# w_o and y of the RWKV projection loaded in the last head pair, without the meetings between; a weight ring of ten chunks

## What is computed

```python
for i in range(DEPTH):                      # DEPTH = 2
    h = rms_norm(x, norm_mix_g[i])
    mix = rwkv7_time_mix(h, ...) if i % 2 == 0 else mla_mix(h, ...)
    x = x + mix                             # both end in "... @ w_o", 1024 x 1024
    x = x + expert_choice_ffn(rms_norm(x, norm_ffn_g[i]), ...)

# the end of rwkv7_time_mix: y is normalised per head of 64
y = ((y - mean) * lax.rsqrt(var + GN_EPS)).reshape(b, s, d)
y = y * gn_g + gn_b + bonus.reshape(b, s, d)
out = (y * g) @ w_o

def expert_choice_ffn(h, w_router, w_gate, w_up, w_down):
    aff = jax.nn.softmax(h @ w_router, axis=-1)          # 512 x 16
    gates, idx = lax.top_k(jnp.swapaxes(aff, 1, 2), cap) # cap = 64 tokens an expert
    xe = h[b_idx, idx]
    hid = jax.nn.silu(xe @ w_gate) * (xe @ w_up)         # w_*: 16 x 1024 x 1024 a layer
    ye = (hid @ w_down) * gates[..., None]
    return jnp.zeros_like(h).at[b_idx, idx].add(ye)
```

## Time and profile before

| what | us |
|---|---|
| median of three runs (lowest, highest) | 2177.22 (2176.36, 2178.32) |
| the profiled execution, its time | 2174.74 |
| its span in the trace | 2172.6 |
| last pair's v projection done on PE, end of the pairs | about 663, 720 |
| layer 0: first matmul of the projection | 743.00 |
| layer 0: PE starts on chunk 0, last chunk read | 845.08, 1295.3 |
| layer 1: projection, PE starts on chunk 0, last chunk read | 1603.30, 1701.7, 2152.0 |
| PE busy (share of the span), mean clock | 1872.0 (86%), 0.955 |
| DVE, ACT, POOL busy | 845.8, 511.7, 228.6 |
| DMA moved, mean rate | 462.01 MB, 213 GB/s |

### The profile page before, as it was taken

The page is one execution under the profiler, slowest core; times in us unless marked ns, Lnnn a source line. Parts: engine busy times, 40 slices in busy tenths (PEclk is TensorE's granted clock), DMA queues, the critical chain, the costliest instruction groups (busy, mean ns, idle before and its releaser), DMA issues.

```text
span 2172.6 us, 43866 instructions
## 1 busy us (share of the span) xinstructions
PE 1872.0 (86%) x19382; PEld 986.8 (45%) x19382; DVE 845.8 (39%) x1685; ACT 511.7 (24%) x989; POOL 228.6 (11%) x264
## 2 busy tenths in 40 slices
PE   3689999999998595999888887699986799989987
PEld 2257766666667342333333324566643333333332
DVE  6557556564654114222212212477733222222211
ACT  1133443453343020111010101355521011001010
POOL 0031133033113020000000000111201000000000
PEclk8899999999999796999999998899998899999999
DMA  3111011011100744999999982200044599999996
GB/s 81 33 34 36 8 36 41 20 29 36 41 8 10 270 200 186 427 427 428 427 426 428 427 343 73 97 22 31 11 184 166 243 427 427 427 428 427 427 428 285
DMA packets 84534, 462.01 MB, mean 213 GB/s; under 512 B 16637, under 2 KB 49786, under 8 KB 59770
## 3 DMA queue, kind: packets, MB, share of 16 engines
q1 hardware_dynamic: 82042, 450.82, 50.8%
q0 software_dynamic: 2304, 8.39, 1.0%
HBM read 451.06 MB, written 8.13 MB: 211 GB/s over the span
## 4 chain that ended last, share of the span: by engine, by line
PE 60%; DMA 19%; DVE 6%; issue 6%; ACT 5%; DVEq 2%; SPq 1%; ACTq 1%; POOLq 0%; POOL 0%; PEldq 0%; another core or an unknown queue 0%
DMA arena<-in_moe_w_down 18%; PE banks L1504 14%; PE bank L602 7%; PE banks L1256 5%; PE banks L769 5%; PE bank L1504 4%; PE bank L1548 3%; PE banks L873 2%; PE banks L1548 2%; ACT arena L1936 2%; PE banks L956 1%; PE banks L459 1%; PE banks L893 1%; PE banks L747 1%; PE banks L1486 1%
## 5 line engine op out<-in xcount | busy, mean ns | idle before, releaser
L1504 PE MATMUL banks<-arena 128*64 128x512 f32 x2560 | 569.9, 598 | 32.7 <-DMA arena<-in_moe_w_up 20.3
L1504 PEld LDWEIGHTS banks<-arena 128*64 128x64 f32 x2560 | 179.0, 137 | 387.8 <-issue 338.4
L602 PE MATMUL bank<-arena 128*128 128x512 f32 x384 | 191.4, 626 | 9.1 <-ACT arena L642 8.0
L1605 DVE TENSOR_TENSOR arena<-arena,bank 128x512 f32<-128x512 f32 x80 | 55.0, 688 | 337.4 <-PE bank L1548 337.4
L1504 PE MATMUL bank<-arena 128*64 128x512 f32 x512 | 118.8, 610 | 38.7 <-issue 25.7
L1104 POOL TENSOR_TENSOR arena<-arena 128x512 f32<-128x512 f32 x80 | 101.6, 1295 | 436.5 <-DVE arena L1159 436.3
L769 PE MATMUL banks<-arena 64*64 64x64 f32 x5632 | 126.8, 221 | 10.1 <-issue 6.9
L769 PEld LDWEIGHTS banks<-arena 64*64 64x64 f32 x5632 | 111.0, 134 | 49.1 <-issue 40.7
L1256 PE MATMUL banks<-arena 128*128 128x512 f32 x256 | 115.3, 607 | 16.1 <-POOLq L379 16.1
L1593 DVE SCALAR_TENSOR_TENSOR arena<-arena,banks 128x512 f32<-128x512 f32 x32 | 33.7, 1053 | 212.6 <-PE banks L1504 212.6
L1560 ACT ACTIVATE arena<-banks 128x512 f32<-128x512 f32 x32 | 19.1, 598 | 413.0 <-PE banks L1504 413.0
(11 more groups left out here) (322 smaller groups left out, 2612.3 us busy)
## 6 DMA issues: line engine op xcount, KB each, us to landing
arena<-in_moe_w_gate SPq DMA_DIRECT2D x64, 2048.0 KB, 35.4
arena<-in_moe_w_up SPq DMA_DIRECT2D x64, 2048.0 KB, 35.4
arena<-in_moe_w_down SPq DMA_DIRECT2D x64, 2048.0 KB, 29.7
out_dram<-arena SPq DMA_DIRECT2D x12, 512.0 KB, 3.5
arena<-in_x SPq DMA_DIRECT2D x8, 512.0 KB, 11.4
arena<-in_rw_wr SPq DMA_DIRECT2D x8, 512.0 KB, 4.2
arena<-in_rw_wk SPq DMA_DIRECT2D x8, 512.0 KB, 6.0
arena<-in_rw_wv SPq DMA_DIRECT2D x8, 512.0 KB, 6.0
```

What stands on the lines that cost most here:

```text
L602: last = nc.tensor.matmul(b[:, :], w_sl[:, n, k, :], xmix[n][:, k, :], start=(k == 0), stop=(k == ND - 1))
L1504: last = nc.tensor.matmul(b[z * CAP:(z + 1) * CAP, :], st[:, k, :], ring[g % RING][:, k, z * 512:(z + 1) * 512], start=(c % 2 == 0 and k = ...
L1605: nc.vector.tensor_tensor(xs, xs, b[:, :], ALU.add).then_inc(free[COMB[j]], 1)
```

## The change

The regions. The ring has ten slots: seven at the arena's end, then `hT`, then `h_tok`, then the 4,096 floats ahead of `RING0`. What routing uses is placed in that last region (`fin`), and what the experts still need of it goes to the small array. For layer 0, w_o and yT get a place of their own over `xmix`, at the arena's end; this covers slots 3 to 6 of the ring.

The front. There are no meetings between the pairs and the projection of layer 0. In the last-but-one pair, once PE has done the v projection, SP issues w_o and, after six stores of y, their load. Pair 6's y goes straight into yT. PE does seven of eight k steps of the first job, the last y's transposes, seven of the second job, then the two last steps. The bank numbers of layer 0's projection go on from those of the pairs.

SP's order around the routing. Chunks 0 to 2 go first (in layer 0 after the last y), 3 and 4 ahead of the last row store (in layer 0 after the last out job), 5 to 7 after it, 8 when the row stores have landed, 9 when the slots have been made (in layer 0 also after a meeting in which SP now takes part, since the semaphores of the pairs are cleared there). At the end the four tiles of x are stored each after its last addition, with no meeting.

```diff
@@ -101,9 +101,10 @@
         ps = [banks06[:, b * 512:(b + 1) * 512] for b in range(6)]
         ps += [ctx.enter_context(nc.psum_tensor(f"bank{b}", [P, 512], F32)) for b in range(6, NB)]
 
-        RING0 = ARENA - (RING - 1) * CHUNK
-        ring = [arena[:, RING0 + s * CHUNK:RING0 + (s + 1) * CHUNK].rearrange("p (k n) -> p k n", k=4)
-                for s in range(RING - 1)]
+        KEPT = 7
+        RING0 = ARENA - KEPT * CHUNK
+        four = lambda v: v.rearrange("p (k n) -> p k n", k=4)
+        ring = [four(arena[:, RING0 + s * CHUNK:RING0 + (s + 1) * CHUNK]) for s in range(KEPT)]
         common = place(0)
         x_sb = common(NT, D)
 
...
@@ -192,12 +193,14 @@
         proj = place(AFTER_H + D)
         wo_sb = proj(ND, D)
         assert proj.at[0] <= RING0
-        yT = hT
+        early = place(ARENA - (3 * ND * S + 4 * S))
+        wo_at = [early(ND, D), wo_sb]
+        yT = [early(ND, S), hT]
 
         y_dram = a["out"][0].rearrange("(k q) (c s) -> k (q c) s", k=NPAIR, c=2)
 
 
-        moe = place(AFTER_H + D)
+        moe = place(AFTER_H)
         xeT = moe(ND, 2 * CAP)
         hidT = [moe(ND, CAP) for _ in range(2)]
         hid = [moe(512) for _ in range(2)]
...
@@ -996,10 +1001,8 @@
                         proj_piece(pe, rj, "v", u, n + 1)
 
         def last_y_pe(pe):
-            pe.wait_ge(ynorm_ready, 1)
-            for t in range(NT):
-                last = nc.tensor.transpose(ps[0][:, t * P:(t + 1) * P], ysq[:, t * P:(t + 1) * P], ident[:, :])
-            last.then_inc(full[0], 1)
+            pe.wait_ge(ynorm_ready, NPAIR)
+            turn(pe, ("yT", NPAIR), lambda m: ysq[:, m * P:(m + 1) * P])
 
         def y_square(act, n):
             act.wait_ge(ycen_ready, n)
...
@@ -1143,10 +1146,12 @@
             nc.vector.tensor_tensor(dst, ytok_flat, gT, ALU.mult).then_inc(ydone_ready, 1)
 
         def last_y_dve(dve):
+            for h in range(2):
+                job_read(dve, rj, ("y", h, NPAIR - 1))
             y_centre(dve)
-            y_variance(dve, 1)
-            y_scale(dve, 1)
-            y_finish(dve, 0, 1, 1, yT[:, NPAIR - 1, :])
+            y_variance(dve, NPAIR)
+            y_scale(dve, NPAIR)
+            y_finish(dve, *rj[("yT", NPAIR)], (NPAIR - 1) % 2, yT[0][:, NPAIR - 1, :])
 
         def pairs_dve(dve):
             for u in range(NPAIR):
...
@@ -1242,20 +1247,21 @@
         for t in range(NT):
             order += [(("out", t, z), (2 * t + z) % 4) for z in range(2)]
             order += [(("tr", t, i), 4 + i) for i in range(2)] + [(("lg", t), 6 + t % 2)]
-        oj = Jobs(order + [("sel", 0), ("at", 1), ("st", 2)])
+        order += [("sel", 0), ("at", 1), ("st", 2)]
+        ojs = [Jobs(order, rj.count), Jobs(order)]
         tile = lambda t: slice(t * P, (t + 1) * P)
 
         def out_pe(pe, n):
+            oj = ojs[n]
             pe.wait_ge(ld_wo[n], 16)
-            if n == 0:
-                pe.wait_ge(ld_y, 16)
-
-            def out(t, z):
-                b = open_job(pe, oj, ("out", t, z))
-                for k in range(ND):
-                    last = nc.tensor.matmul(b[:, :], yT[:, k, tile(t)], wo_sb[:, k, z * 512:(z + 1) * 512],
+
+            def out(t, z, ks=range(ND)):
+                b = open_job(pe, oj, ("out", t, z)) if 0 in ks else ps[oj[("out", t, z)][0]]
+                for k in ks:
+                    last = nc.tensor.matmul(b[:, :], yT[n][:, k, tile(t)], wo_at[n][:, k, z * 512:(z + 1) * 512],
                                             start=(k == 0), stop=(k == ND - 1))
-                last.then_inc(full[oj[("out", t, z)][0]], 1)
+                if ND - 1 in ks:
+                    last.then_inc(full[oj[("out", t, z)][0]], 1)
 
             def turn_x(t):
                 pe.wait_ge(x_ready, t + 1)
...
@@ -1282,8 +1288,19 @@
                 if t == NT - 1:
                     last.then_inc(full[oj["sel"][0]], 1)
 
-            out(0, 0)
-            out(0, 1)
+            if n == 0:
+
+                pe.wait_ge(ld_y, 16)
+                pe.wait_ge(ydone_ready, NPAIR - 1)
+                out(0, 0, range(ND - 1))
+                last_y_pe(pe)
+                out(0, 1, range(ND - 1))
+                pe.wait_ge(ydone_ready, NPAIR)
+                for z in range(2):
+                    out(0, z, range(ND - 1, ND))
+            else:
+                for z in range(2):
+                    out(0, z)
             pe.wait_ge(router_ready, 1)
             for t in range(1, NT):
                 out(t, 0)
...
@@ -1441,7 +1461,7 @@
             nc.vector.tensor_copy(token_f, token_i)
             b = job_full(dve, oj, "st")
             nc.vector.tensor_copy(slot[:, :, 0:NE], b[:, 0:NT * NE].rearrange("p (t e) -> p t e", t=NT))
-            dve.drain()
+            dve.drain().then_inc(routed[layer], 1)
             picks(dve, 0)
 
         def picks(dve, first):
...
@@ -1623,14 +1644,29 @@
 
         def load_experts(sp, layer):
 
-            for g in range(RING - 1):
+            if layer == 0:
+                sp.wait_ge(ydone_ready, NPAIR)
+            for g in range(3):
                 load_chunk(sp, layer, g)
             rows = h_dram.rearrange("(t p) d -> p t d", p=P)
             for t in range(NT):
+                if t == NT - 1:
+                    if layer == 0:
+                        job_full(sp, ojs[0], ("out", NT - 1, 1))
+                    load_chunk(sp, layer, 3)
+                    load_chunk(sp, layer, 4)
                 sp.wait_ge(h_done[layer], t + 1)
                 sp.dma_start(rows[:, t, :], h_tok[:, t, :]).then_inc(h_stored[layer], 16)
+            load_chunk(sp, layer, 5)
+            load_chunk(sp, layer, 6)
             sp.wait_ge(hT_read[layer], 1)
-            load_chunk(sp, layer, RING - 1)
+            load_chunk(sp, layer, KEPT)
+            sp.wait_ge(h_stored[layer], 16 * NT)
+            load_chunk(sp, layer, KEPT + 1)
+            if layer == 0:
+                meet(sp, "sp")
+            sp.wait_ge(routed[layer], 1)
+            load_chunk(sp, layer, KEPT + 2)
             for g in range(RING, CPP * PAIRS):
                 chunk_read(sp, layer, g - RING)
                 load_chunk(sp, layer, g)
...
@@ -2027,9 +2063,7 @@
             meet_pool(pool, [consts_ready])
             meet_pool(pool, prep_sems, everyone)
             pairs_pool(pool)
-            meet_pool(pool, pairs_sems, everyone)
-            y_rstd(pool, 1)
-            meet_pool(pool, banks + y_sems, everyone)
+            y_rstd(pool, NPAIR)
             for layer in range(2):
                 if layer == 1:
                     norm_pool(pool)
...
@@ -2041,9 +2075,13 @@
                     attn_pool(pool)
                     meet_pool(pool, attn_sems, everyone)
                 out_pool(pool, layer)
-                meet_pool(pool, route_sems)
+                if layer == 0:
+                    meet_pool(pool, route_sems + [x for x in pairs_sems if x not in banks], everyone)
+                else:
+                    meet_pool(pool, route_sems)
                 moe_pool(pool, layer)
-                meet_pool(pool, moe_sems, everyone)
+                if layer == 0:
+                    meet_pool(pool, moe_sems, everyone)
 
         @block.tensor
         def _(pe):
...
@@ -2056,9 +2094,6 @@
             first_pe(pe)
             meet(pe, "pe")
             pairs_pe(pe)
-            meet(pe, "pe")
-            last_y_pe(pe)
-            meet(pe, "pe")
             for layer in range(2):
                 if layer == 1:
                     norm_pe(pe)
...
@@ -2153,9 +2187,10 @@
             pair_loads(sp, 0)
             gate_loads(sp, 0)
             meet(sp, "sp")
+            wo = [a[w][0].rearrange("(k p) n -> p k n", p=P) for w in ("rw_wo", "mla_w_o")]
             pair_loads(sp, 1)
             for u in range(NPAIR):
-                if u:
+                if 0 < u < NPAIR - 1:
                     sp.wait_ge(ydone_ready, u)
                     sp.dma_start(y_dram[u - 1], y_out[u % 2]).then_inc(y_stored, 16)
                 sp.wait_ge(full[rj[("g", u)][0]], rj[("g", u)][1])
...
@@ -2164,18 +2199,16 @@
                     sp.wait_ge(full[rj[("v", u)][0]], rj[("v", u)][1])
                 if u < NPAIR - 2:
                     pair_loads(sp, u + 2)
-            sp.wait_ge(y_stored, 16 * (NPAIR - 1))
-            sp.sem_inc(waited_sp, 1)
-            meet(sp, "sp")
+                if u == NPAIR - 2:
+                    sp.dma_start(wo_at[0], wo[0]).then_inc(ld_wo[0], 16)
+                    sp.wait_ge(y_stored, 16 * (NPAIR - 2))
+                    sp.dma_start(yT[0][:, 0:NPAIR - 2, :], y_dram[0:NPAIR - 2].rearrange("k p s -> p k s")).then_inc(ld_y, 16)
             sp.wait_ge(ld_pair, LOADS * NPAIR)
             sp.wait_ge(ld_gate, 16 * 2 * NPAIR)
-            sp.dma_start(yT[:, 0:NPAIR - 1, :], y_dram[0:NPAIR - 1].rearrange("k p s -> p k s")).then_inc(ld_y, 16)
-            wo = [a[w][0].rearrange("(k p) n -> p k n", p=P) for w in ("rw_wo", "mla_w_o")]
```

(5 more changed lines are left out.)

63 lines of the change are left out of this document (34 added, 29 removed).

## The result

The changed kernel took 2139.35 us (median of four runs, 2135.06 to 2141.43) beside 2177.06 for the kernel before (four runs); the ratio is 0.9826, 95% interval 0.9811 to 0.9840, 37.7 us less. A repeat with five runs gave 2138.11 and 0.9815 (0.9802 to 0.9829), 39.7 us less. The profiled execution took 2135.06, its span 2133.3.

A forecast was written before the change was run, and what follows sets the result against it. It took DMA streaming expert weights at 427 GB/s as the main bound, besides SP's queue before the projection. Terms summed to -44.9 us, from 2174.74 to 2129.8 profiled; with 2.5 to the median, 2132.3, range 2127 to 2143.

The forecast's parts named there:

- five signs of being wrong: PE idle before job three; first gather 8 us or more; expert DMA below 420; w_down not ending the chain; longer last pair.
- late router: Rival, layer 0's projection: router columns or x come late, PE stands before job three up to 4 us; 2136 us, chance 0.11.
- crowding: Rival, routing: both first gathers pay the whole 6.2 us and PE or DVE stands once per layer; 2147 us, chance 0.12.
- signs of being right: Projection near 720 without cold stretch, second job 735.2, chunk 0 near 823, refill to landing 435 us, last addition 4 before end.
- The front: Pairs to layer 0's projection: early w_o and y loads and no meetings bring the second job forward, -24.7 us.
- The first gather of layer 0: Routing, layer 0: the gather meets the chunk stream for some 4 us and lands when it drains, +2.0 us, bounds 0 and 6.2.
- The ring: Expert stages: ten chunks resident at the first read leave two fewer to stream, -9.8 us in each layer.
- The first gather of layer 1: Routing, layer 1: the gather meets the end of chunk 9's transfer, +1.0 us, bounds 0 and 6.2.
- The end: End of the span: three tiles' stores go ahead and only the last is left after the last addition, -3.9 us.
- slower rival: Expert stream: ten transfers in flight run at a lower rate than eight; 2226 us at 10% less, chance 0.02.

The follow-up runs named there:

- wo_late: The changed kernel with w_o loaded after the last y matmul, not under the last pair: 9.3 us slower than the changed kernel on the same chip.
- wo_twice: The changed kernel with w_o loaded twice in the last pair, the second time when the first has landed: 34.9 us less than the kernel before.
- ring8: The changed kernel with a ring of eight slots in place of ten: 24.6 us less than the kernel before.
- end_meet: The changed kernel with the last meeting back and the four stores of x behind it: 34.4 us less than the kernel before.
- before_a: The kernel before, unaltered, timed and profiled once more: 2180.24 us.
- before_b: The kernel before, unaltered, timed and profiled yet again: 2181.18 us.

## Why the prediction was right, and where it was off

The range, 2127 to 2143, held both medians, and the path of the forecast is the one that happened. But the time lies 7 us above the forecast of 2132.3, and two of the five signs of being wrong were seen: a first gather of 8 us or more (9.7), and a last pair longer because of its loads. The range held because it had been drawn wide for a late router, which didn't come, and for most of the crowding, which came in part; that the cost of the w_o load, for which no case had a price, fitted into it too is luck. The signs of being right came in kind, each up to some 6 us late: the first projection matmul at 723.6 without a cold stretch, the second job taken at 738.2, PE on chunk 0 at 828.6, the last addition 3.1 us before the end; from the first refill to the last landing are 435.4 and 435.6 us, as said. By its own steps:

1. The front. Forecast -24.7 from the shift of the second job. Counted from the y copy it is 15.1 in place of 40.25, -25.1; PE didn't stop, the clock stayed at 1.00, and the router was ready 2.8 us ahead of job three, so "late router" didn't come. What failed is the sentence that 13.6 us of transfer "lie under that work": the cover costs. The step gave the w_o load no price, and it measured +3.8 us (66.7 against 63.0), shown by wo_late and wo_twice. PE waits there for blocks of its code that land late.
2. The first gather of layer 0. Forecast +2.0 with bounds 0 and 6.2; measured 8.7 to 9.7 in six kernels with chunk 9 beside it against 4.4 to 4.7 in eight without, +4.5. The step reasoned that it meets the stream for only some 4 us and lands when that drains. The queue was longer than that: chunk 8 was to be in at about 813 and landed at 819.68, 3.4 us of that from the later y copy, and chunk 9 at 825.5, where 818 was said. So the gather had 9.3 us of stream beside it, and landed 0.3 us behind chunk 9 (0.3 to 0.6 in all six kernels). The Trainium skill, "DMA: Bandwidth & Descriptors", section "Queues, rings and completion order", lets each engine take turns between its rings packet by packet. The prediction worked out +1.2 us from equal shares, saw that the median of 10.8 is far above that, and supposed unequal packets without putting a size to them. The trace has the size: a packet of the chunk is four times as large as one of the gather (14 and 3.6 KB above). Turns of one packet each would put 2.0 MB of chunk beside the gather's 0.52, 4.8 us at 427 GB/s; that is an estimate, and it is near the +4.5. In its timing the trace agrees only in part: the gather's packets are spread over 4.6 us in place of 2.3, but the first of them also starts late, 4.7 us after the issue in place of 1.9 (4.3 to 4.7 in all six, 1.9 in the eight others), and nothing here shows why.
3. The ring, -9.8 in each layer: -10.9 and -10.0 in the first pair of profiles, and 9.7 and 10.0 lost again in ring8 by the mean of the others. The arithmetic of two chunks at 4.91 us was right, and DMA stayed at 427 GB/s with ten chunks in flight, so the slower rival fell.
4. The first gather of layer 1, +1.0: 4.81 against 4.39, +0.4.
5. The end, -3.9: 20.63 to 16.08, -4.6, and end_meet gives it back.

With the measured terms (the 0.2 lies between the second addition and the gather's issue) the sum is 3.8 - 25.1 + 0.2 + 5.0 - 10.9 - 10.0 + 0.4 - 4.6 = -41.2 against -39.3 in the spans of the first two profiles; the difference is the drift between the layers (294.4 and 296.2), which also shows in before_a and before_b. The forecast of -44.9 missed by the unpriced w_o load (3.8) and 3.0 of the first gather, less 2.0 us that the ring and the end gave beyond their terms and 1.1 of the front, the second gather and the meeting; the drift comes on top. That makes 5.3 us in the profiled execution (2135.06 against 2129.8). The other 1.8 are between it and the median: 4.3 us this time, where the prediction took the 2.5 of the kernel before. "Crowding" at 2147 was named as what could make up such a difference, and in part it did: the first gather of layer 0 paid most of its price, that of layer 1 nearly none. The stops it foresaw once a layer didn't come; what PE lost, it lost ahead of the routing, in the pair.

## What to carry to other kernels

Deepening a ring in front of a stream that is at its ceiling is worth the bytes it moves ahead of the first read (9.7 and 10.0 us for two chunks of 4.91), and nothing for the stream itself. A transfer put under work isn't free because that work doesn't wait for it: where PE runs through code of many small matmuls, its own instructions come over the same DMA engines, and spreading the load in pieces with pauses gave half of the cost back. And ask which short transfer is waited for next before filling idle DMA time: one 2 MB chunk held back for a 0.5 MB gather gave 5 us at no cost.
